# Down projection of a decoder layer as seven products of half matrices in place of eight

## The reference

```python
def layer(x, ...):
    h = rmsnorm(x, g_pre_mix)
    z = h @ w_in                                   # 1024 -> 4608: a | u | v | gate a | gate b
    ...
    x = x + rmsnorm(m @ w_out, g_post_mix)         # 1024 -> 1024
    f = jnp.square(jax.nn.relu(rmsnorm(x, g_pre_ffn) @ w_up)) @ w_down   # 1024 -> 4096 -> 1024
    x = x + rmsnorm(f, g_post_ffn)
```

## Time and profile before

| | |
|---|---|
| median of 3 runs | 3723.31 us |
| lowest, highest | 3722.25, 4476.52 us |
| profiled execution | 3722.54 us |
| span of its slowest core | 3721.5 us |
| PE, DVE, ACT, POOL busy | 3686.8, 1761.9, 1158.7, 551.2 us |

### The profile page before, as it was taken

How to read it: one execution, slowest core, us unless ns; L and a number is a source line. 1 busy time by engine, 2 the same in 40 slices (tenths; PEclk the granted TensorE clock), 3 DMA queues, 4 the chain that set the end, 5 groups by cost and what they waited for, 6 DMA issues and landing times.

```text
span 3721.5 us, 64208 instructions; the slowest of 8 cores (3710.7 to 3721.5 us)
## 1 busy us (share of the span) xinstructions
PE 3686.8 (99%) x22338; PEld 2110.8 (57%) x22338; DVE 1761.9 (47%) x3378; ACT 1158.7 (31%) x2528; POOL 551.2 (15%) x1228
## 2 busy tenths in 40 slices
PE   8999999999999999999999999999999999999999
PEld 4554555555455555545555554555665665665664
DVE  3642662564365256335525633552562662653652
ACT  2331332333133232323323232332332332332331
POOL 1111110111111021111102111111120211211110
PEclk9999999999999999999999999999999999999999
DMA  8583765658376576837646674765877877776773
GB/s 168 93 148 69 121 114 97 114 98 153 59 134 113 103 162 110 143 68 131 116 87 111 111 140 75 131 119 94 177 154 128 152 143 130 141 146 124 150 122 81
DMA packets 78860, 449.35 MB, mean 121 GB/s; under 512 B 9680, under 2 KB 13392, under 8 KB 32592
## 3 DMA queue, kind: packets, MB, share of 16 engines
q0 software_dynamic: 59392, 385.48, 60.6%
q1 hardware_dynamic: 19152, 59.76, 5.6%
HBM read 817.55 MB, written 13.10 MB: 223 GB/s over the span
## 4 chain that ended last, share of the span: by engine, by line
PE 97%; DMA 1%; DVE 1%; issue 1%; POOL 0%; ACT 0%; SPq 0%; DVEq 0%; POOLq 0%; ACTq 0%
PE ps L393 88%; PE ps L952 6%; PE ps L448 2%; PE ps L831 1%; DMA wpg<-w_pg 1%; DMA wslot<-wslab 0%; DMA x<-xp 0%; DVE hst L440 0%; PE ps L373 0%; POOL stt L413 0%; DVE ps L906 0%; DVE x L935 0%; POOL wslot L311 0%; POOL R L883 0%; DVE R L851 0%
## 5 line engine op out<-in xcount | busy, mean ns | idle before, releaser
L393 PE MATMUL ps<-hTb,wslot 128*128 128x384 bf16 (+1 forms) x11520 | 1840.3, 317 | 3.8 <-DVE R L851 1.9
L393 PEld LDWEIGHTS ps<-hTb,wslot 128*128 128x128 bf16 x11520 | 1120.0, 98 | 648.1 <-issue 11.1
L393 PE MATMUL ps<-wslot,R 128*128 128x512 bf16 x4352 | 947.3, 379 | 0.0
L402 ACT ACTIVATE R<-ps 128x384 bf16<-128x384 f32 (+5 forms) x1208 | 577.6, 483 | 915.5 <-PE ps L393 865.9
L393 PEld LDWEIGHTS ps<-wslot,R 128*128 128x128 bf16 x4352 | 424.3, 98 | 503.0
L970 DVE TENSOR_TENSOR R<-R 128x384 bf16<-128x384 bf16 (+1 forms) x768 | 266.7, 347 | 587.6 <-ACT R L402 586.2
L393 PE MATMUL ps<-R,wslot 128*128 128x384 bf16 (+1 forms) x2304 | 406.8, 317 | 0.0
L311 POOL DMA_DIRECT2D wslot<-wslab x360 | 199.6, 557 | 890.6 <-PE ps L393 736.9
L402 ACT ACTIVATE sg<-ps 128x384 bf16<-128x384 f32 (+1 forms) x384 | 179.9, 473 | 460.4 <-PE ps L393 255.0
L393 PEld LDWEIGHTS ps<-R,wslot 128*128 128x128 bf16 x2304 | 223.8, 98 | 125.2 <-issue 0.9
L440 DVE SCALAR_TENSOR_TENSOR hst<-x,stt,gpre 128x1024 bf16<-128x1024 f32 x136 | 174.6, 1283 | 168.1 <-POOL stt L413 166.0
(11 more groups left out here) (79 smaller groups left out, 1941.5 us busy)
## 6 DMA issues: line engine op xcount, KB each, us to landing
wslot<-wslab POOLq DMA_DIRECT2D x359, 1024.0 KB, 16.6
x<-xp SPq DMA_DIRECT2D x16, 512.0 KB, 12.6
yp<-x SPq DMA_DIRECT2D x16, 512.0 KB, 6.6
gpre<-g_pre_m SPq DMA_DIRECT2D x12, 512.0 KB, 13.9
gpre<-g_pre_f SPq DMA_DIRECT2D x12, 512.0 KB, 13.0
gpost<-g_pm SPq DMA_DIRECT2D x12, 512.0 KB, 20.6
gpost<-g_pf SPq DMA_DIRECT2D x12, 512.0 KB, 4.5
R<-b_sp SPq DMA_DIRECT2D x22, 256.0 KB, 10.1
```

The costliest lines, as they stand in the source:

```text
L393: r = e.matmul(ps[b][:, 0:N], lhsT=lh, rhs=rh, start=(at + q == 0), stop=(at + q == total - 1))
L402: lambda e: e.activation(out=out, in_=in_, func=func, **kw), cost=act_us(N))
```

## The change

The inner dimension (32 chunks) is cut into a low and a high half of 16 chunks, the output columns into two halves, and the first 2 x NP tiles into a low and a high half of NP tiles (NP = NT // 2: 3, or 2 with the fifth tile left over). With B11, B21 the low and high inner half of w_down for the first output columns, B12, B22 for the second, each two slabs, the four results of a block product come from seven products, each NP tiles x 16 matmuls of 512 columns. They run in seven passes:

| pass | left side | right side | bank |
|---|---|---|---|
| 1 | P5 = high tokens, low + high chunks | B22 | Z, copied to hst |
| 2 | high tokens, low chunks | B12 - B22 | Z, goes on |
| 3 | low tokens, high chunks | B21 - B11 | Y, copied to og0 |
| 4 | E0 = low tokens, low + high chunks | B11 | Y, goes on |
| 5 | low tokens, high chunks + high tokens, low chunks | B11 + B22 | X, copied to hTb |
| 6 | low tokens - high tokens, low chunks | B11 + B12 | X, goes on |
| 7 | high tokens - low tokens, high chunks | B21 + B22 | W |

The sums of weights are made by DVE in the slots themselves (`wsum`, L1052 of the new kernel), five times two slabs a layer; the sums of activations by DVE into R1, hTb and fT itself (`fsum`, L1042), twenty a layer. They are rounded to bf16. Copies of open banks are made by ACT (`snap`, L1093), sums between results by DVE on the banks (L1170, L1193, L1207, L1236) and by POOL in SBUF (L1181, L1184, L1204, 512 fp32 each). The order of the w_down slabs changes, and all eight are held until pass 4 has ended; they are released two by two after passes 4, 5, 6 and 7. The low tiles are finished after pass 6, their chains emitted in full before the high tiles are closed (L1236), whose chains are emitted with the next layer's groups. `add_eps` moves from the first half of the down projection into the chain. The preparation of the next layer's spatial weights (`prep`) moves from the second half of the up projection to the first half's second pass. In block 2 `subs` becomes 256 and 384.

The diff, cut; of the second half only what is new stands here, the loops that it replaces are those of the kernel before.

```diff
+DN_ORDER = [SL_DN + q for q in (0, 1, 6, 7, 4, 5, 2, 3)]
+SLAB_ORDER = list(range(SL_DN)) + DN_ORDER
...
+                    if has_next and s8 < 3:
+                        prep(nsamp, s8, parR)
...
+                E0 = hTb[:, 0:16 * H].rearrange("p (c t) -> p c t", c=16)
+                E0f = hTb[:, 0:512 * 2 * NP].bitcast(F32).rearrange("p (a f) -> p a f", a=NP)
+                P5 = R1[:, 0:8 * H].bitcast(BF16).rearrange("p (c t) -> p c t", c=16)
...
+                def fsum(out, ko, c0, h0, c1, h1, op, n=4):
+                    sl = (LO, HI)
+                    S.op("dve", fk(c0, h0, n) + fk(c1, h1, n), ko,
+                         lambda e: e.tensor_tensor(out=out, in0=fT[:, c0:c0 + n, sl[h0]], in1=fT[:, c1:c1 + n, sl[h1]],
+                                                   op=op), cost=dve_us(n * H, 1.7))
...
+
+                    for q in range(2):
+                        ko, wo = slab(bi, l, SL_DN + o + q)
+                        ka, wa = slab(bi, l, SL_DN + a_ + q)
+                        kb, wb = slab(bi, l, SL_DN + b_ + q)
+                        S.op("dve", [ka, kb], [ko],
+                             lambda e: e.tensor_tensor(out=wo[:, :], in0=wa[:, :], in1=wb[:, :], op=op), cost=2.45)
+
+                B11, B21, B12, B22 = 0, 2, 4, 6
+
...
+                    for q in range(2):
+                        kw, sv = slab_kn(bi, l, SL_DN + w + q, 8)
+                        for k0 in (0, 4):
+                            pace()
+                            CH.pump()
+
+                            def emit(e):
+                                for k in range(k0, k0 + 4):
+                                    r = e.matmul(ps[b][:, :], lhsT=lhs(8 * q + k, p), rhs=sv[:, k, :],
+                                                 start=(start and q == 0 and k == 0), stop=(q == 1 and k == 7),
+                                                 skip_group_check=not start)
+                                return r
+                            S.op("pe", [kw] + lkeys(8 * q + k0), [("ps", b)], emit, cost=mm_us(4, 512))
+                    CH.pump(False)
+
+                def cols_of(c0, h):
...
+                    xk = xslot(bi, i)
+                    yield S.ready(("st", i, 0), ("st", i, 1)), False
+                    add_eps(i)
+                    rs_post(i)
+                    yield S.ready(("st", i, 3)), False
...
                     for jj in range(4):
                         for n in range(2):
                             up_group(s8, jj, n)
                     release(bi, l, SL_UP + s8)
-                    if has_next and s8 in (4, 5, 6):
-                        prep(nsamp, s8 - 4, parR)
-
-
-                for i in range(NT):
-                    n = 0 if i < 3 else 1
+                    k = 4 * (s8 - 4)
+                    fsum(P5[:, k:k + 4, :], KR + PARK + [("p5", k)], k, 1, 16 + k, 1, add)
+                    fsum(fT[:, 16 + k:20 + k, HI], fk(16 + k, 1), 16 + k, 1, 16 + k, 0, sub)
...
+                if NT == 5:
+                    std_tile(1)
+                Zb, Yb, Xb, Wb = {}, {}, {}, {}
+                for k in range(0, 16, 4):
+                    fsum(E0[:, k:k + 4, :], KE + [("e0", k)], k, 0, 16 + k, 0, add)
+                wsum(B12, B12, B22, sub)
+                for p in range(NP):
+                    Zb[p] = b = bank()
+                    prod(p, b, lambda c, p: P5[:, c, 128 * p:128 * p + 128],
+                         lambda c: [("p5", c)] + (KR if c == 12 else []), B22, True)
+                    snap(b, hstf[p], [("hst", p)])
+                if NT == 5:
+                    std_tile(0)
+                wsum(B21, B21, B11, sub)
+                for k in range(0, 16, 4):
+                    fsum(fT[:, k:k + 4, LO], fk(k, 0), k, 0, k, 1, sub)
+                f, fkk = cols_of(0, 1)
+                for p in range(NP):
+                    b = Zb[p]
+                    prod(p, b, f, fkk, B12, False)
+                    S.op("dve", [("hst", p)], [("ps", b), ("nb", p)],
+                         lambda e, b=b, p=p: e.tensor_tensor(out=nb[p][:, :], in0=ps[b][:, :], in1=hstf[p], op=sub),
                          cost=dve_us(512))
+                    square(b, NP + p, 1)
+                    og_mul(b, og12[p][0], [og12[p][1]], 1)
+                f, fkk = cols_of(16, 0)
+                wsum(B22, B11, B22, add)
+                for p in range(NP):
+                    Yb[p] = b = bank()
+                    prod(p, b, f, fkk, B21, True)
+                    snap(b, og0[:, p, :], [("og0", p)])
+                    S.op("pool", [("og0", p)], [("nb", p)],
+                         lambda e, p=p: e.tensor_tensor(out=nb[p][:, :], in0=nb[p][:, :], in1=og0[:, p, :], op=add),
+                         cost=1.2)
+                    S.op("pool", [("og0", p)], [("hst", p)],
+                         lambda e, p=p: e.tensor_tensor(out=hstf[p], in0=og0[:, p, :], in1=hstf[p], op=sub), cost=1.2)
+                for k in range(0, 16, 4):
+                    fsum(fT[:, 16 + k:20 + k, LO], fk(16 + k, 0), k, 1, 16 + k, 0, add)
+                wsum(B12, B12, B22, add)
+                for p in range(NP):
+                    b = Yb[p]
+                    prod(p, b, lambda c, p: E0[:, c, 128 * p:128 * p + 128],
+                         lambda c: [("e0", c)] + (KE if c == 12 else []), B11, False)
+                    S.op("dve", [], [("ps", b), ("nb", p)],
+                         lambda e, b=b, p=p: e.tensor_tensor(out=nb[p][:, :], in0=nb[p][:, :], in1=ps[b][:, :], op=sub),
+                         cost=dve_us(512))
+                    square(b, p, 0)
+                    og_mul(b, q4(og0[:, p, :]), [("og0", p)], 0)
+                release_w(B11)
+                f, fkk = cols_of(16, 0)
+                for p in range(NP):
+                    Xb[p] = b = bank()
+                    prod(p, b, f, fkk, B22, True)
+                    snap(b, E0f[:, p, :], KE)
+                    S.op("pool", KE + [("hst", p)], [("r1", p)] + fk(4 * p, 1),
+                         lambda e, p=p: e.tensor_tensor(out=r1v[p], in0=q4(E0f[:, p, :]), in1=q4(hstf[p]), op=add),
+                         cost=1.2)
+                    S.op("dve", [("nb", p)], [("ps", b)],
+                         lambda e, b=b, p=p: e.tensor_tensor(out=ps[b][:, :], in0=ps[b][:, :], in1=nb[p][:, :], op=add),
+                         cost=dve_us(512))
+                    if p == 0:
+                        wsum(B21, B21, B22, add)
+                release_w(B22)
+                if NT == 5:
+                    finish(4, [(0, q4(og0[:, 5, :]), ("og0", 5)), (512, q4(nb[2][:, :]), ("nb", 2))])
                 if last and has_next:
                     for i in range(3):
                         launch(i, lambda i=i: start_norm(i, xslot(nbi, i), nV["hT"]))
 
+                f, fkk = cols_of(0, 0)
+                for p in range(NP):
+                    b = Xb[p]
+                    prod(p, b, f, fkk, B12, False)
+                    square(b, p, 1)
+                    og_mul(b, og22[p], [("og22", p)] + fk(16 + 4 * p, 0), 1)
+                    finish(p, [(0, q4(og0[:, p, :]), ("og0", p)), (512, og22[p], ("og22", p))])
+                release_w(B12)
+                f, fkk = cols_of(16, 1)
+                for p in range(NP):
+                    Wb[p] = b = bank()
+                    prod(p, b, f, fkk, B21, True)
+                release_w(B21)
+                for p in range(NP):
+                    CH.flush(ffn[p] if last else hT_chain[p])
+                for p in range(NP):
+                    b, i = Wb[p], NP + p
+                    S.op("dve", [("r1", p)], [("ps", b)],
+                         lambda e, b=b, p=p: e.tensor_tensor(out=q4(ps[b][:, :]), in0=q4(ps[b][:, :]), in1=r1v[p], op=add),
+                         cost=dve_us(512))
+                    square(b, i, 0)
+                    og_mul(b, q4(nb[p][:, :]), [("nb", p)], 0)
+                    finish(i, [(0, q4(nb[p][:, :]), ("nb", p)), (512,) + og12[p]])
```

184 lines of the change are left out of this document (105 added, 79 removed).

## The result

| | before | after |
|---|---|---|
| median of the runs | 3724.2 us | 3786.9 us |
| ratio of undisturbed runs | 1 | 1.0165 (95%: 1.0142 to 1.0188) |
| profiled execution, span | 3721.5 us | 3786.1 us |
| granted clock, all cores | 0.997 to 0.998 | 0.982 to 0.987 |
| PE busy | 3686.8 us | 3611.7 us |

The forecast was 3661 us, the range ended at 3715: too low by 126 us, and on the wrong side of no change.

The account below looks back on a forecast made before the run. PE was taken as the bound, busy 3686.8 of 3721.5 us. 3722.5 - 110.5 + 15.2 + 11.2 + 10.4 + 10.5 + 1.3 = 3660.6, so 3661 us as median; range 3630 to 3715.

Parts of the forecast that it names:

- Removed: Down projections over twelve layers: 512 matmuls of 512 columns go at 0.2159 us each, 110.5 us, all on the path.
- Added on DVE: Weight, activation and bank sums in the down projection: hidden with six tiles; waits of 3.8 us a five-tile layer, 15.2 in all.
- Nothing is late: Six-tile down projection: DVE's sums and closings are ready when PE wants them, 0 us.
- The unknown: POOL's additions beside DVE: Third and fifth passes: POOL may hold DVE, from 0 to 1.18 us each; half taken, 11.2 us, all in five-tile layers.
- half is shown: Reason for charging half: rows show POOL held by DVE (0.57 to 1.43 us), none shows whether DVE is held.
- the first rival: POOL's additions in the down projection hold DVE in full: 38.4 us with six tiles, 38.4 with five; 3711 us, chance 0.18.
- With six tiles half still hides: Six-tile layers, POOL holding DVE by half: second bank addition comes at 55.4 us, wanted at 55.3, so no cost.
- At nothing: the weights: Down slabs: the last lands 8.2 to 15.7 us after its request, DVE wants it at 13; no cost.
- Moved: Boundaries of layers: tile chains hide only behind the last pass; 10.4 us with six tiles, 10.5 with five, 1.3 at the end.
- Layer boundaries inside a block: Waits at transposes and bank ps6 where layers meet: 1.3 us a six-tile layer, 3.5 a five-tile one.
- The clock: A clock that falls after waits was named as a sign that the forecast is wrong; no size was given.
- the forecast's own terms for late DVE and for boundaries: 15.2 us of five-tile DVE waits; layer boundaries 10.4 and 10.5 us, and 1.3 at the last layer's end.

## Why the prediction was wrong, step by step

- **Removed, 110.5 us.** Right: L1065 and L396 have 3840 matmuls of 512 columns from the halves of R and hTb.
- **Added on DVE.** The prices were right (2.28, 0.955, 0.69 when POOL is still). "Nothing is late" with six tiles was right: without the additions no wait at the bank addition is left in blocks 0 and 1. With five tiles 2.2 + 1.6 us were forecast, 1.8 + 1.4 measured.
- **The unknown: POOL's additions beside DVE. This step failed.** I took half because "half is shown". The rows showed POOL held by DVE and no case in which DVE could be held; that is no evidence for half. It was nearly the first rival, in full: in one layer DVE lost 2.2 us at two slab sums, 4.3 at four activation sums and 1.6 at the two slab sums of the fifth pass, 8.1 for nine additions where the price in full was 9 x 1.18 = 10.6. The term stood in the sum with 11.2 us and measured 78: a layer inside blocks 0 and 1 took 318.4 us in the mean and 312.7 to 313.8 without the additions, and block 2 alone gave about 21. "With six tiles half still hides" failed with it. The waits at the bank additions came near the first rival's, 0.92 + 2.97 us with six tiles (4.8) and 4.60 + 1.28 with five (5.9 + 2.8). The Trainium skill, page "SBUF — State Buffer", section "Who interferes with whom", says that the two contend and, of DVE's two-port modes, that the first to issue holds the ports for the whole instruction; for these sums of two SBUF inputs the 6.67 us against 4.48 agree in the direction that was open.
- **At nothing: the weights. This failed too.** I checked the last of the eight slabs against DVE (wanted at 13) and no other against PE. With six tiles that was right: PE waits for no slab there. With five the unsplit tile wants the fifth and sixth slabs at t = 0, and in each layer of block 2 PE stood there, 3.2 to 5.1 us. Half the bytes gave 24 us back in three layers and 17 at the boundary ahead of them. What makes the fifth and sixth slabs land that late in a five-tile layer no run shows.
- **At nothing: no term for the block boundaries.** "Moved" followed the chains of a layer boundary. The same move puts store and load of x on the path at two places, 21 and 37 us over the forecast: the store starts 10 us ahead of the end of the down projection instead of 30, and the load takes longer. The key that the diff widened is 18 of the 33.6 us of wait at the second, of which 10 came back. The diff shows both (`i == 2` for `i + 2`, `+ KX`, `+ KO`); neither was in the sum.
- **The start.** `NG = 8` was in the diff and the earlier trace rows had 11.8 us of waits at the start. Its 22 us came the other way and by luck hid a part of the miss, which without them is 148 us.
- **Layer boundaries inside a block.** Right in size: 0.6 to 1.5 us with six tiles (forecast 1.3), 0.6 + 1.6 + 0.9 with five (3.5).
- **The clock.** It was named as what would make the forecast wrong, and priced at nothing. PE was busy some 35 us longer than the matmuls need, but a part of this would have been waiting otherwise; how large a part is open.

The sign was wrong because four costs were missing or too small at once. Slower than before needed costs over the ceiling of 110.5 us; with the 22 us of the start they came to 196. Measured each in its own kernel, POOL's additions are 78, the slabs 40, the stores 22 and the key 10; the forecast's own terms for late DVE and for boundaries were another 37. That adds up to 187, in which the slabs and the key overlap at the head of block 2. The slabs, the stores and the key had no rival of their own.

What stays open: how the 24 us of the slabs inside block 2 divide into waits and slower matmuls behind them, and how much of a boundary is the slower load of x.

## What to carry to other kernels

Removing matmuls in one pattern also removes what hid behind them: list every store, load and key that changes place, and follow it across the outermost loop's boundary, not only the inner one's. Two elementwise engines on shared memory are priced as one until a row shows otherwise; moving nine additions a layer from the idle engine to the loaded one was worth 50 us. Check every weight against its first reader, not the last weight alone. Apply such a scheme where its cover exists: against the kernel of before with eight semaphores it gave some 43 us (1.2%) in 6 of 12 layers, and lost 85 (2.3%) in all 12.

## What was not expected of the hardware

A DVE sum of two SBUF tensors and a POOL addition lengthen each other: 2.28 to 3.3 us a slab sum at worst, 0.95 to 1.95 an activation sum, 1.26 to 3.3 a POOL addition. They end in step, one for one. And the same wait of 3 us of PE was followed by a lower granted clock in five layers (0.52 from 327.20 to 330.60 us) and by 1.00 in three, while a wait of 0.7 us in the same place was followed by 1.00 in all eight.
